# Tokens in residue order: two attention groups score 128 keys instead of 256

## The chip, the cores and the metric

The kernel runs on one core of a Trainium2 chip. The metric is the device time of one execution in microseconds (us), as the median of several runs. The trace shown is of one profiled execution. The engines are TensorE (PE; its weight loads are PEld), VectorE (DVE), ScalarE (ACT), GpSimd (POOL) and SyncE (SP).

## What is computed

A two-layer encoder on 256 tokens of width 1024, in float32. Each layer has a mixer and a feed-forward part; layer 0 has a dense SwiGLU, layer 1 eight experts of which each token uses two. The mixer reads one normalised input through one wide projection into two branches: a recurrence over time (convolution of width 4, then a gated linear scan forward and backward), and attention. In the attention, 12 heads of 64 channels are in three groups of four. Group g has a dilation d and a window: a query at t sees the keys t + j*d.

```python
WINDOWS = (128, 512, 2048)
DILATIONS = (1, 4, 16)
def dilated_band_attention(q, k, v, dilation, half_keys):
    """Query t attends keys t + j*dilation, j in [-half_keys, half_keys]."""
    ...
    s = jnp.einsum('brnqhd,brnkhd->brnhqk', qb, kb) * (HEAD_DIM ** -0.5)
    ...
    s = jnp.where(mask[None, None, :, None, :, :], s, -jnp.inf)
    lse = jax.nn.logsumexp(s, axis=-1)
    ...
mix = jax.nn.softmax(jnp.stack(lses, axis=0), axis=0)
att = jnp.sum(mix[..., None] * jnp.stack(outs, axis=0), axis=0)
```

The three groups are weighed by their denominators, so that slot s (one head of each group) is one softmax over the allowed keys of its three heads. With 256 tokens the two wider windows cut nothing off: their groups see every key of the query's own residue mod 4 or mod 16.

## The kernel before

Tokens lie on partitions in two blocks (TB = 2) of 128, in the order of time. All weights come from HBM as one stream of 1 MB parts into the ring `raw`, loaded by SP. Each part has two halves; a half is split in two for accuracy: ACT writes `w_hi` (L478), DVE the rest `w_lo` (L485), three halves ahead of PE. PE makes three matmuls for each product (`mm3`, L490 to L492: hi by hi, lo, and lo by hi).

The order of all work is one list, `STEPS`, that `schedule()` writes out by hand. Every engine goes through it and does its own share of each step. A step "G" is one half of a product with weights; `at(gap, ...)` puts side steps between the products. The side steps that matter here:

- "tx": PE transposes the recurrence's input, DVE copies it from PSUM into `xT` (L1367). "conv" (L1375, L1382) makes `xc` from `xT` shifted by 0 to 3 tokens; "lg" is the recurrence's gates, fp32 matmuls on `xc` (L994), whose 256 columns per product go to the PSUM tile `mid`. "ls" are the scans (L1414, L1418), whose result goes back to `xT`, and "lf" multiplies it with `gy` (L1431).
- "tq": queries and keys transposed into `qkT`.
- The attention has 8 units a layer, u = token block x slot. "as" is the scores of a unit (L1020): for each of three groups one fp32 matmul, 64-row weights (the 128 queries of the block), all 256 keys as columns, into `mid` (768 columns over two banks). "am": DVE adds the mask `band` and takes the maximum (L1453), ACT takes the exponential with its sum (L802), all on 128x768 in `sm`. "ap" transposes four 128-column pieces of `sm` on PE (L1030), and ACT copies them to `pt` (L808); "aq" transposes the other two, and DVE copies those (L1464) and takes the reciprocal of the sum (L1468). "av" multiplies the six pieces with `v`, six fp32 matmuls of 64 columns (L1043), and DVE scales the result into `att` (L1474).

These stages of different units share a slot between two products: `stages = [("ap", i - 2), ("as", i), ("av", i - 3), ("aq", i - 2), ("am", i)]` (L144). The transposed results of "tn", "tx", "tq", "ap", "aq", "av" and others take turns on two PSUM banks, `turn`, in the order of the list: a step waits until the last but one user of its bank was read. `mid` is single: the scores of a unit wait until the masking pass of the unit before has read it.

The masks are part of the constants that ACT's queue loads at the start (L668): two blocks x three groups x 256 columns, 0 or -1e30.

Of the kernel before, what the change touches and what calls it, by code (L numbers as in the profile page):

```python
# [35 lines left out]
UNITS = TB * SLOTS  # L36
F_DENSE, F_EXP, EXPERTS = 2816, 3584, 8
EPS = 1e-6
SCALE = DH ** -0.5
NEG = -1e30  # L40
# [48 lines left out]
def schedule():  # L89
# [16 lines left out]
    for L in range(DEPTH):  # L106
# [35 lines left out]

        for i in range(UNITS + 3):
            stages = [("ap", i - 2), ("as", i), ("av", i - 3), ("aq", i - 2), ("am", i)]  # L144
            at(20.5 + i / 2, *(s for s in stages if 0 <= s[1] < UNITS))
# [59 lines left out]
def tables():  # L205


    half_at, last_half, pair, freed, kinds = {}, {}, {}, {}, {}

    uses, ring = [0, 0, 0], {2: 0, 3: 1}  # L210
    todo = []
    for L in range(DEPTH):
        todo += [((L, n), k, i, 2) for n, k, i in MIXER]
        if L == 0:
            todo += [((L, n), k, i, 3) for n, k, i in dense_order()]
    for j, (key, kind, i, width) in enumerate(todo):
        half_at[key, i], last_half[key] = 2 * j, 2 * j + 2
        if key not in kinds:
            kinds[key] = kind
            pair[key], freed[key] = [], []  # L220
            for _ in range(2 if kind in "ws" else 1):
                if key[1][0] == "lru":
                    p = 2
                else:
                    p = ring[width] % width
                    ring[width] += 1
                pair[key].append(p)
                freed[key].append(uses[p])
                uses[p] += TB
    turn, n = {}, 0  # L230
    count = {"tn": 2, "tx": 2, "ty": 2, "tq": 1, "ap": 1, "aq": 1, "av": 1, "ta": 1, "tm": 2, "th": 2}
# [14 lines left out]
C_MASK = 4 * P  # L246
C_COS = C_MASK + TB * GROUPS * T
C_SIN = C_COS + TB * 8
# [29 lines left out]
def build(nc, stream, gates_w, x_in, norms, consts_in, vecs_in, out):  # L278
    with ExitStack() as ctx:
        def keep(name, shape, dt=F32, into=ctx):  # L280
            return into.enter_context(nc.sbuf_tensor(name, shape, dt))
# [21 lines left out]
        with ExitStack() as m:  # L303
            sm = keep("sm", [P, 2, GROUPS * T], into=m)
            pt = [keep("pt0", [P, 2 * GROUPS, P], into=m)]
            att = keep("att", [P, TB, T], into=m)
            with ExitStack() as m2:
                pt.append(keep("pt1", [P, 2 * GROUPS, P], into=m2))
            att_hi = keep("att_hi", [P, 2, T], F32R, m)
            att_lo = keep("att_lo", [P, 2, T], F32R, m)  # L310
# [198 lines left out]
        def mid_before(L, use):  # L509


            lru = min(use, 8)
            at_ = use - lru
            return L * 16 + use, L * (8 * 4 + 8) + 4 * lru + at_

        def xslice(n):
# [117 lines left out]
        def _(act):  # L634
# [28 lines left out]
            for s in STEPS:  # L663
# [141 lines left out]
                elif kind == "ap":  # L805
                    idx = TURN[s]
                    bank_full(act, idx)
                    nc.scalar.activation(pt[s[2] % 2][:, 0:4, :],  # L808
                                         turn[idx % 2][:, :].rearrange("p (a t) -> p a t", a=4),
# [89 lines left out]
        def _(pe):  # L899
# [37 lines left out]
            for s in STEPS:  # L937
# [70 lines left out]
                elif kind == "as":  # L1008
                    _, L, u = s
                    b, sl = u // SLOTS, u % SLOTS  # L1010
                    uses, frees = mid_before(L, 8 + u)
                    pe.wait_ge(mid_free, frees)
                    if u == 0:
                        for j in range(4, 6):
                            bank_read(pe, TURN[("tq", L, j)])
                    flat = mid[:, :, :].rearrange("p a c -> p (a c)")
                    for g in range(GROUPS):
                        head = g * SLOTS + sl
                        o = DH * (head % 2)
                        ins = nc.tensor.matmul(flat[:, g * T:(g + 1) * T],  # L1020
                                               qkT[o:o + DH, head // 2, 0, b * P:(b + 1) * P],
                                               qkT[o:o + DH, head // 2, 1, :], start=True, stop=True)
                    ins.then_inc(mid_full, 1)
                elif kind in ("ap", "aq"):

                    _, L, u = s
                    pe.wait_ge(p_ready, 8 * L + u + 1)
                    t_ = turn_bank(TURN[s])
                    for k, c in enumerate(range(4) if kind == "ap" else range(4, 2 * GROUPS)):
                        ins = nc.tensor.transpose(t_[:, k * P:(k + 1) * P], sm[:, u % 2, c * P:(c + 1) * P],  # L1030
                                                  ident)
                    ins.then_inc(turned, 1)
                elif kind == "av":
                    _, L, u = s
                    b, sl = u // SLOTS, u % SLOTS
                    for part in ("ap", "aq"):
                        bank_read(pe, TURN[(part, L, u)])
                    idx = TURN[s]
                    t_ = turn_bank(idx)
                    for i in range(2 * GROUPS):  # L1040
                        g, kb = i // 2, i % 2
                        o = (g * SLOTS + sl) * DH
                        ins = nc.tensor.matmul(t_[:, 0:DH], pt[u % 2][:, i, :], v[:, kb, o:o + DH],  # L1043
                                               start=i == 0, stop=i == 2 * GROUPS - 1)
                    ins.then_inc(turned, 1)
# [154 lines left out]
        def _(dve):  # L1200
# [65 lines left out]
            for s in STEPS:  # L1266
# [94 lines left out]
                elif kind == "tx":  # L1361
                    _, L, c = s
                    for k in range(2):
                        idx = TURN[s] + k
                        n = 4 * c + 2 * k
                        bank_full(dve, idx)
                        nc.vector.tensor_copy(xT[:, n:n + 2, 1:T + 1],  # L1367
                                              turn[idx % 2][:, :].rearrange("p (n t) -> p n t", n=2)
                                              ).then_inc(turn_free[idx % 2], 1)
# [55 lines left out]
                elif kind == "lf":  # L1425
                    _, L, pr = s
                    dve.wait_ge(scanned, scans_done(L, 1, 1))
                    for i in range(2):
                        bank_read(dve, TURN[("ty", L, 1)] + i)
                    y2 = gy[:, 2 * pr:2 * pr + 2, :]  # L1430
                    nc.vector.tensor_tensor(y2, xT[:, 2 * pr:2 * pr + 2, 0:T], y2,  # L1431
                                            ALU.mult).then_inc(lru_full, 1)
# [11 lines left out]
                elif kind == "am":  # L1444
# [4 lines left out]
                    if u >= 2:  # L1449

                        bank_full(dve, TURN[("aq", L, u - 2)])
                    flat = mid[:, :, :].rearrange("p a c -> p (a c)")
                    nc.vector.tensor_tensor_reduce(out=sm[:, u % 2, :], in0=flat[:, 0:GROUPS * T],  # L1453
                                                   in1=band[:, b, :], scale=1.0, scalar=NEG, op0=ALU.add,
# [4 lines left out]
                                            ALU.mult).then_inc(nm_ready, 1)  # L1459
                elif kind == "aq":  # L1460
                    _, L, u = s
                    idx = TURN[s]
                    bank_full(dve, idx)
                    nc.vector.tensor_copy(pt[u % 2][:, 4:6, :],  # L1464
                                          turn[idx % 2][:, 0:2 * P].rearrange("p (a t) -> p a t", a=2)
                                          ).then_inc(turn_free[idx % 2], 1)
                    dve.wait_ge(p_ready, 8 * L + u + 1)
# [251 lines left out]


def constants():

    c = np.zeros((P, C_END), np.float32)
    i = np.arange(P)
    c[:, C_ID:C_ID + P] = np.eye(P)
    c[:, C_IOTA:C_IOTA + P] = i[None, :]
    c[:, C_BEFORE:C_BEFORE + P] = i[:, None] < i[None, :]
    c[:, C_ONES:C_ONES + P] = 1
    k = np.arange(T)
    for b in range(TB):  # L1730
        rel = (b * P + i)[:, None] - k[None, :]
        for g in range(GROUPS):
            ok = (rel % DILATIONS[g] == 0) & (np.abs(rel) <= WINDOWS[g] // 2)
            o = C_MASK + (b * GROUPS + g) * T
            c[:, o:o + T] = np.where(ok, 0, NEG)
        freq = (np.float32(500000.0) ** (-np.arange(0, 16, 2, dtype=np.float32) / np.float32(16))).astype(np.float32)
        ang = (b * P + i)[:, None].astype(np.float32) * freq[None, :]
# [37 lines left out]
```

## Time and profile before

| | us |
|---|---|
| runs, median of 3 | 1754.05 |
| runs, lowest and highest | 1750.28, 1754.47 |
| profiled execution, first to last instruction | 1745.8 |
| PE busy in it | 1695.2 |
| DVE busy | 1410.3 |
| ACT busy | 1223.3 |
| POOL busy | 45.1 |

For the profiled execution the span is what is given; it runs from the first to the last instruction, and a run's device time holds what lies around it as well. An engine's busy time is an average over stages with different limits, so it must be read stage by stage. The attention of layer 0 lies at about 160 to 220 us, that of layer 1 at 600 to 660 us, and the experts take the time from about 720 us to the end.

### The profile page before, as it was taken

What the parts mean: (1) busy time and instruction counts of PE and PEld (TensorE: products, weight loads), DVE (VectorE), ACT (ScalarE), POOL (GpSimd) and SP (SyncE); (2) the same over time, 40 slices, a digit from 0 to 9 for tenths busy, and PEclk for the clock granted to TensorE, in tenths of its full rate; (3) what the DMA queues carried; (4) which work ended last, traced back from release to release, by engine and by line L of the source; (5) the groups of instructions that cost most, each with busy time, mean ns of one, the idle gap of its engine ahead of it and who ended that gap; (6) DMA issues with size and microseconds to landing.
All of it is one profiled execution on the core that took longest, in us unless ns stands there. A gap on an engine that the chain in (4) does not pass through costs nothing.

```text
span 1745.8 us, 24050 instructions
## 1 busy us (share of the span) xinstructions
PE 1695.2 (97%) x7960; PEld 1397.6 (80%) x7960; DVE 1410.3 (81%) x1546; ACT 1223.3 (70%) x1431; POOL 45.1 (3%) x30
## 2 busy tenths in 40 slices
PE   7989999999999999899999999999999999999996
PEld 5877888888887788688888888888888888888885
DVE  5777575565777756699899899899898998998997
ACT  5686545444568754578878878777787877888785
POOL 0130000000003000000000000000000000000000
PEclk9999999999999999899999999999999999999999
DMA  9434255555543324299899899899899998998993
GB/s 366 167 121 145 97 217 205 185 183 187 189 146 136 145 97 168 97 365 371 329 367 368 328 362 375 324 367 371 322 368 347 349 369 339 352 373 326 368 369 137
DMA packets 66120, 471.22 MB, mean 270 GB/s; under 512 B 7312, under 2 KB 7568, under 8 KB 9744
## 3 DMA queue, kind: packets, MB, share of 16 engines
q1 hardware_dynamic: 64768, 462.97, 70.4%
q0 software_dynamic: 864, 6.29, 1.0%
q10 hardware_dynamic: 432, 1.22, 0.2%
q8 instruction: 34, 0.56, 0.1%
q14 instruction: 22, 0.18, 0.0%
HBM read 469.41 MB, written 1.05 MB: 269 GB/s over the span
## 4 chain that ended last, share of the span: by engine, by line
PE 86%; DVE 6%; ACT 5%; issue 2%; DMA 1%; SPq 0%; DVEq 0%; ACTq 0%
PE bank L490 18%; PE bank L492 18%; PE bank L491 18%; PE mid L490 8%; PE mid L492 8%; PE mid L491 8%; PE turn L1118 2%; PE turn L1159 1%; PE mid L1020 1%; PE turn L1043 1%; DVE w_lo L485 1%; DMA raw<-in_stream 1%; ACT w_hi L478 1%; DVE xT L1414 1%; PE mid L994 1%
## 5 line engine op out<-in xcount | busy, mean ns | idle before, releaser
L485 DVE TENSOR_TENSOR w_lo<-raw,w_hi 128x1024 fp32r<-128x1024 f32 x877 | 1069.7, 1234 | 241.4 <-ACT w_hi L478 201.0
L478 ACT ACTIVATE w_hi<-raw 128x1024 fp32r<-128x1024 f32 x877 | 924.3, 1060 | 326.4 <-PE bank L492 194.3
L490 PE MATMUL bank<-w_hi,g_hi 128*128 128x512 f32 x896 | 357.2, 399 | 0.0
L492 PE MATMUL bank<-w_hi,g_lo 128*128 128x512 f32 x896 | 351.3, 392 | 0.0
L491 PE MATMUL bank<-w_lo,g_hi 128*128 128x512 f32 x896 | 351.2, 392 | 0.0
L490 PE MATMUL bank<-w_hi,a_hi 128*128 128x512 f32 (+1 forms) x608 | 242.3, 399 | 14.9 <-DVE w_lo L485 12.2
L492 PE MATMUL bank<-w_hi,a_lo 128*128 128x512 f32 (+1 forms) x608 | 235.0, 387 | 0.0
L491 PE MATMUL bank<-w_lo,a_hi 128*128 128x512 f32 (+1 forms) x608 | 234.5, 386 | 0.0
L490 PEld LDWEIGHTS bank<-w_hi,g_hi 128*128 128x128 f32 x896 | 168.8, 188 | 38.1 <-DVE w_lo L485 3.0
L492 PEld LDWEIGHTS bank<-w_hi,g_lo 128*128 128x128 f32 x896 | 168.5, 188 | 38.1
L491 PEld LDWEIGHTS bank<-w_lo,g_hi 128*128 128x128 f32 x896 | 168.9, 189 | 34.3
L490 PE MATMUL mid<-w_hi,eT_hi 128*128 128x512 f32 x448 | 178.1, 398 | 0.0
L492 PE MATMUL mid<-w_hi,eT_lo 128*128 128x512 f32 x448 | 175.7, 392 | 0.0
L491 PE MATMUL mid<-w_lo,eT_hi 128*128 128x512 f32 x448 | 174.8, 390 | 0.0
L490 PEld LDWEIGHTS bank<-w_hi,a_hi 128*128 128x128 f32 x608 | 116.2, 191 | 40.9 <-issue 15.9
L492 PEld LDWEIGHTS bank<-w_hi,a_lo 128*128 128x128 f32 x608 | 115.9, 191 | 23.4
L491 PEld LDWEIGHTS bank<-w_lo,a_hi 128*128 128x128 f32 x608 | 116.5, 192 | 21.2
L492 PEld LDWEIGHTS mid<-w_hi,eT_lo 128*128 128x128 f32 x448 | 84.1, 188 | 19.1
L491 PEld LDWEIGHTS mid<-w_lo,eT_hi 128*128 128x128 f32 x448 | 84.3, 188 | 17.5
L490 PEld LDWEIGHTS mid<-w_hi,eT_hi 128*128 128x128 f32 x448 | 84.3, 188 | 16.7
L802 ACT ACTIVATE sm<-sm,small 128x768 f32<-128x768 f32 x16 | 15.0, 939 | 45.6 <-DVE small L1458 45.6
L1623 DVE TENSOR_TENSOR eT_lo<-turn,eT_hi 128x512 fp32r<-128x512 f32 x56 | 38.3, 683 | 0.0
(224 smaller groups left out, 1608.0 us busy)
## 6 DMA issues: line engine op xcount, KB each, us to landing
raw<-in_stream SPq DMA_DIRECT2D x438, 1024.0 KB, 4.8
wg<-in_gates POOLq DMA_DIRECT2D x2, 2048.0 KB, 11.8
gain<-in_norms POOLq DMA_DIRECT2D x4, 512.0 KB, 4.0
x<-in_x SPq DMA_DIRECT2D x2, 512.0 KB, 6.0
raw<-in_stream SPq DMA_DIRECT2D x2, 512.0 KB, 6.7
out_x<-xn SPq DMA_DIRECT2D x4, 256.0 KB, 2.1
const<-in_consts ACTq DMA_DIRECT2D x1, 1008.0 KB, 14.0
gain<-in_norms SPq DMA_DIRECT2D x2, 256.0 KB, 7.0
```

The costliest lines, as they stand in the source:

```text
L478: nc.scalar.activation(w_hi[:, h % H, :], raw[:, part % R, lo:lo + HALF], ACT.Copy).then_inc(hi_ready, 1)
L485: nc.vector.tensor_tensor(w_lo[:, h % H, :], raw[:, part % R, lo:lo + HALF], w_hi[:, h % H, :].bitcast(F32), ALU.subtract).then_inc(lo_rea ...
L490: nc.tensor.matmul(out_, s_hi, wh, start=start, stop=False)
L491: nc.tensor.matmul(out_, s_hi, wl, start=False, stop=False)
L492: return nc.tensor.matmul(out_, s_lo, wh, start=False, stop=stop)
L994: ins = nc.tensor.matmul(mid[:, q, g * T:(g + 1) * T], wg[:, d, g, n, :], xc[:, n, :], start=True, stop=True)
L1020: ins = nc.tensor.matmul(flat[:, g * T:(g + 1) * T], qkT[o:o + DH, head // 2, 0, b * P:(b + 1) * P], qkT[o:o + DH, head // 2, 1, :], start ...
L1043: ins = nc.tensor.matmul(t_[:, 0:DH], pt[u % 2][:, i, :], v[:, kb, o:o + DH], start=i == 0, stop=i == 2 * GROUPS - 1)
L1118: ins = nc.tensor.matmul(t_[:, k * P:(k + 1) * P], src[:, b, kt * P:(kt + 1) * P], sel[:, b, :], start=i == 0, stop=i == 2 * TB - 1)
L1159: ins = nc.tensor.transpose(t_[:, k * P:(k + 1) * P], eh[c % 2][:, k * P:(k + 1) * P], ident)
L1414: nc.vector.tensor_tensor_scan(xT[:, n, 0:T], rg[:, n, :], ig[:, n, :], 0.0, ALU.mult, ALU.add).then_inc(scanned, 1)
L1623: nc.vector.tensor_tensor(eT_lo[c % 2][:, :, :], turn[idx % 2][:, :].rearrange("p (k t) -> p k t", k=4), eT_hi[c % 2][:, :, :].bitcast(F32 ...
```

## The change

The host hands the tokens over in another order: all t with t mod 4 = 0 first, then 1, 2, 3 (`token_order`), and puts the output back into the order of time. Block 0 holds residues 0 and 1, block 1 residues 2 and 3. A query of the groups with dilation 4 and 16 then finds all its keys in its own block, so "as" has 256 + 128 + 128 = 512 columns for a unit instead of 768, which is one bank of `mid`; units alternate between the two banks (`att_free`). "am" works on 512 columns, "aq" is gone, "av" has four products, and the mask has 512 columns a block. The rotary tables and the group with dilation 1 follow the new order through tables and mask. The recurrence needs the order of time: "tx" writes `xT` back into it, and "lf" reads it out of it, by an access pattern with a step of four elements (`by_residue`).

```diff
-            stages = [("ap", i - 2), ("as", i), ("av", i - 3), ("aq", i - 2), ("am", i)]
+            stages = [("ap", i - 2), ("as", i), ("av", i - 3), ("am", i)]
...
+        def att_free(L, u):
+
+            return mid_before(L, 8)[1] if u < 2 else mid_before(L, 8 + u - 1)[1]
+
+        def by_residue(a):
+
+            return a.rearrange("p n (j r) -> p n r j", r=RES)
...
-                    nc.scalar.activation(pt[s[2] % 2][:, 0:4, :],
+                    nc.scalar.activation(pt[s[2] % 2][:, :, :],
...
-                    pe.wait_ge(mid_free, frees)
+                    pe.wait_ge(mid_free, att_free(L, u))
...
-                    for g in range(GROUPS):
+                    own = slice(b * P, (b + 1) * P)
+                    for g, keys, o_ in ((0, slice(0, T), 0), (1, own, T), (2, own, T + P)):
                         head = g * SLOTS + sl
                         o = DH * (head % 2)
-                        ins = nc.tensor.matmul(flat[:, g * T:(g + 1) * T],
-                                               qkT[o:o + DH, head // 2, 0, b * P:(b + 1) * P],
-                                               qkT[o:o + DH, head // 2, 1, :], start=True, stop=True)
+                        ins = nc.tensor.matmul(mid[:, u % 2, o_:o_ + keys.stop - keys.start],
+                                               qkT[o:o + DH, head // 2, 0, own],
+                                               qkT[o:o + DH, head // 2, 1, keys], start=True, stop=True)
...
-                    for k, c in enumerate(range(4) if kind == "ap" else range(4, 2 * GROUPS)):
+                    for c in range(KEYS // P):
...
-                    for i in range(2 * GROUPS):
-                        g, kb = i // 2, i % 2
+                    for i, (g, kb) in enumerate(((0, 0), (0, 1), (1, b), (2, b))):
...
-                        nc.vector.tensor_copy(xT[:, n:n + 2, 1:T + 1],
-                                              turn[idx % 2][:, :].rearrange("p (n t) -> p n t", n=2)
+                        nc.vector.tensor_copy(by_residue(xT[:, n:n + 2, 1:T + 1]),
+                                              turn[idx % 2][:, :].rearrange("p (n r j) -> p n r j", n=2, r=RES)
...
-                    nc.vector.tensor_tensor(y2, xT[:, 2 * pr:2 * pr + 2, 0:T], y2,
+                    y4 = y2.rearrange("p n (r j) -> p n r j", r=RES)
+                    nc.vector.tensor_tensor(y4, by_residue(xT[:, 2 * pr:2 * pr + 2, 0:T]), y4,
...
-                        bank_full(dve, TURN[("aq", L, u - 2)])
-                    flat = mid[:, :, :].rearrange("p a c -> p (a c)")
-                    nc.vector.tensor_tensor_reduce(out=sm[:, u % 2, :], in0=flat[:, 0:GROUPS * T],
+                        bank_full(dve, TURN[("ap", L, u - 2)])
+                    nc.vector.tensor_tensor_reduce(out=sm[:, u % 2, :], in0=mid[:, u % 2, :],
...
-                elif kind == "aq":
+                elif kind == "ap":
                     _, L, u = s
-                    idx = TURN[s]
-                    bank_full(dve, idx)
-                    nc.vector.tensor_copy(pt[u % 2][:, 4:6, :],
-                                          turn[idx % 2][:, 0:2 * P].rearrange("p (a t) -> p a t", a=2)
-                                          ).then_inc(turn_free[idx % 2], 1)
+                    if u >= 2:
+                        bank_read(dve, TURN[("av", L, u - 2)])
                     dve.wait_ge(p_ready, 8 * L + u + 1)
                     link(nc.vector.reciprocal(rr[:, u % 2:u % 2 + 1], rs[:, u % 2:u % 2 + 1]))
...
+def token_order():
+
+
+    return np.arange(T).reshape(T // RES, RES).transpose().reshape(T)
```

## Rows read from the trace of the kernel before

**Rows 1.** The page: moved bytes in 40 slices, and the chain of waits

```profile
GB/s 366 167 121 145 97 217 205 185 183 187 189 146 136 145 97 168 97 365 371 329 367 368 328 362 375 324 367 371 322 368 347 349 369 339 352 373 326 368 369 137
...
PE 86%; DVE 6%; ACT 5%; issue 2%; DMA 1%; SPq 0%; DVEq 0%; ACTq 0%
```

**Rows 2.** Windows: busy us of PE, PEld, DVE, ACT, POOL (instructions), PE clock, DMA share, GB/s

```profile
40.00:70.00 30.00, 29.07 (x137) 24.53 (x138) 30.00 (x51) 15.17 (x24) 5.98 (x1) 1.00 0.43 161
160.00:220.00 60.00, 59.60 (x325) 48.41 (x324) 33.57 (x69) 36.24 (x54) 0.00 (x0) 1.00 0.26 92
600.00:660.00 60.00, 59.60 (x326) 48.39 (x325) 33.97 (x68) 36.54 (x54) 0.00 (x0) 1.00 0.26 90
760.00:1740.00 980.00, 971.76 (x4480) 799.29 (x4478) 894.88 (x855) 776.40 (x819) 0.00 (x0) 1.00 0.91 346
```

**Rows 3.** Waits: who waited for whom, us in total, times, longest

```profile
ACT w_hi L478 <- DMA raw<-in_stream: 10.2, 3, 6.9
...
PE turn L1030 <- ACT pt L808: 0.8, 2, 0.4
```

**Rows 4.** Timeline of PE in three attention slots: start, us, instruction

```profile
161.72 0.39 PE L491 MATMUL bank<-w_lo,a_hi 128*128 128x512 f32 x1
161.95 0.39 PE L492 MATMUL bank<-w_hi,a_lo 128*128 128x512 f32 x1
162.26 1.56 PE L1020 MATMUL mid<-qkT 64*128 64x256 f32 x6
...
164.09 0.39 PE L491 MATMUL bank<-w_lo,a_hi 128*128 128x512 f32 x1
...
170.83 0.40 PE L492 MATMUL bank<-w_hi,a_lo 128*128 128x512 f32 x1
...
173.08 0.44 PE L1030 MATMUL turn<-const,sm 128*128 128x128 f32 x2
...
173.59 0.39 PE L491 MATMUL bank<-w_lo,a_hi 128*128 128x512 f32 x1
...
175.89 0.40 PE L492 MATMUL bank<-w_hi,a_lo 128*128 128x512 f32 x1
...
179.99 0.39 PE L491 MATMUL bank<-w_lo,a_hi 128*128 128x512 f32 x1
```

**Rows 5.** The chain in order of time: start, us on the chain, what

```profile
62.75 1.73 PE mid L994 x8
...
845.34 1.73 PE turn L1118 x16
```

**Rows 6.** Groups by line: busy us, mean ns, idle before

```profile
L1453 DVE CUSTOM_DVE_ANT_0 sm<-mid,const 128x768 f32<-128x768 f32 x16 | 15.3, 958 | 0.4
...
L1418 DVE TENSOR_TENSOR_SCAN root<-rg,ig 128x256 f32<-128x256 f32 x16 | 9.7, 670 | 0.0
...
L1367 DVE COPY xT<-turn 128x512 f32<-128x512 f32 x8 | 5.1, 682 | 0.8 <-PE turn L981 0.8
```

**Rows 7.** DMA issues (KB each, us to landing), and ACT's timeline at the start

```profile
const<-in_consts ACTq DMA_DIRECT2D x1, 1008.0 KB, 14.0
...
23.38 1.06 ACT L478 ACTIVATE w_hi<-raw 128x1024 fp32r<-128x1024 f32 x1 [6.87 <-DMA raw<-in_stream]
```

**Rows 8.** Timelines of DVE and PE: convolutions and the gates that take them

```profile
45.56 2.46 DVE L1382 SCALAR_TENSOR_TENSOR xc<-xT,vec,xc 128x256 f32<-128x256 f32 x6
...
52.05 2.46 DVE L1382 SCALAR_TENSOR_TENSOR xc<-xT,vec,xc 128x256 f32<-128x256 f32 x6
...
48.21 1.89 PE L994 MATMUL mid<-xc,wg 128*128 128x256 f32 x8
...
55.39 1.89 PE L994 MATMUL mid<-xc,wg 128*128 128x256 f32 x8
...
489.51 2.46 DVE L1382 SCALAR_TENSOR_TENSOR xc<-xT,vec,xc 128x256 f32<-128x256 f32 x6
...
494.29 1.89 PE L994 MATMUL mid<-xc,wg 128*128 128x256 f32 x8
```

More of the change, by code:

```diff
@@ L36 @@
 UNITS = TB * SLOTS
+KEYS = T + 2 * P
+RES = 4
 F_DENSE, F_EXP, EXPERTS = 2816, 3584, 8
@@ L230, in tables @@
     turn, n = {}, 0
-    count = {"tn": 2, "tx": 2, "ty": 2, "tq": 1, "ap": 1, "aq": 1, "av": 1, "ta": 1, "tm": 2, "th": 2}
+    count = {"tn": 2, "tx": 2, "ty": 2, "tq": 1, "ap": 1, "av": 1, "ta": 1, "tm": 2, "th": 2}
     for s in STEPS:
@@ L246 @@
 C_MASK = 4 * P
-C_COS = C_MASK + TB * GROUPS * T
+C_COS = C_MASK + TB * KEYS
 C_SIN = C_COS + TB * 8
@@ L303, in build @@
         with ExitStack() as m:
-            sm = keep("sm", [P, 2, GROUPS * T], into=m)
-            pt = [keep("pt0", [P, 2 * GROUPS, P], into=m)]
+            sm = keep("sm", [P, 2, KEYS], into=m)
+            pt = [keep(f"pt{i}", [P, KEYS // P, P], into=m) for i in range(2)]
             att = keep("att", [P, TB, T], into=m)
-            with ExitStack() as m2:
-                pt.append(keep("pt1", [P, 2 * GROUPS, P], into=m2))
             att_hi = keep("att_hi", [P, 2, T], F32R, m)
@@ L1010, in _ @@
                     b, sl = u // SLOTS, u % SLOTS
-                    uses, frees = mid_before(L, 8 + u)
-                    pe.wait_ge(mid_free, frees)
+                    pe.wait_ge(mid_free, att_free(L, u))
                     if u == 0:
@@ L1015, in _ @@
                             bank_read(pe, TURN[("tq", L, j)])
-                    flat = mid[:, :, :].rearrange("p a c -> p (a c)")
-                    for g in range(GROUPS):
+                    own = slice(b * P, (b + 1) * P)
+                    for g, keys, o_ in ((0, slice(0, T), 0), (1, own, T), (2, own, T + P)):
                         head = g * SLOTS + sl
                         o = DH * (head % 2)
-                        ins = nc.tensor.matmul(flat[:, g * T:(g + 1) * T],
-                                               qkT[o:o + DH, head // 2, 0, b * P:(b + 1) * P],
-                                               qkT[o:o + DH, head // 2, 1, :], start=True, stop=True)
+                        ins = nc.tensor.matmul(mid[:, u % 2, o_:o_ + keys.stop - keys.start],
+                                               qkT[o:o + DH, head // 2, 0, own],
+                                               qkT[o:o + DH, head // 2, 1, keys], start=True, stop=True)
                     ins.then_inc(mid_full, 1)
-                elif kind in ("ap", "aq"):
+                elif kind == "ap":
                     _, L, u = s
@@ L1028, in _ @@
                     t_ = turn_bank(TURN[s])
-                    for k, c in enumerate(range(4) if kind == "ap" else range(4, 2 * GROUPS)):
-                        ins = nc.tensor.transpose(t_[:, k * P:(k + 1) * P], sm[:, u % 2, c * P:(c + 1) * P],
+                    for c in range(KEYS // P):
+                        ins = nc.tensor.transpose(t_[:, c * P:(c + 1) * P], sm[:, u % 2, c * P:(c + 1) * P],
                                                   ident)
@@ L1035, in _ @@
                     b, sl = u // SLOTS, u % SLOTS
-                    for part in ("ap", "aq"):
-                        bank_read(pe, TURN[(part, L, u)])
+                    bank_read(pe, TURN[("ap", L, u)])
                     idx = TURN[s]
                     t_ = turn_bank(idx)
-                    for i in range(2 * GROUPS):
-                        g, kb = i // 2, i % 2
+                    for i, (g, kb) in enumerate(((0, 0), (0, 1), (1, b), (2, b))):
                         o = (g * SLOTS + sl) * DH
                         ins = nc.tensor.matmul(t_[:, 0:DH], pt[u % 2][:, i, :], v[:, kb, o:o + DH],
-                                               start=i == 0, stop=i == 2 * GROUPS - 1)
+                                               start=i == 0, stop=i == KEYS // P - 1)
                     ins.then_inc(turned, 1)
@@ L1449, in _ @@
                     if u >= 2:
-                        bank_full(dve, TURN[("aq", L, u - 2)])
-                    flat = mid[:, :, :].rearrange("p a c -> p (a c)")
-                    nc.vector.tensor_tensor_reduce(out=sm[:, u % 2, :], in0=flat[:, 0:GROUPS * T],
+                        bank_full(dve, TURN[("ap", L, u - 2)])
+                    nc.vector.tensor_tensor_reduce(out=sm[:, u % 2, :], in0=mid[:, u % 2, :],
                                                    in1=band[:, b, :], scale=1.0, scalar=NEG, op0=ALU.add,
@@ L1459, in _ @@
                                             ALU.mult).then_inc(nm_ready, 1)
-                elif kind == "aq":
+                elif kind == "ap":
                     _, L, u = s
-                    idx = TURN[s]
-                    bank_full(dve, idx)
-                    nc.vector.tensor_copy(pt[u % 2][:, 4:6, :],
-                                          turn[idx % 2][:, 0:2 * P].rearrange("p (a t) -> p a t", a=2)
-                                          ).then_inc(turn_free[idx % 2], 1)
+                    if u >= 2:
+                        bank_read(dve, TURN[("av", L, u - 2)])
                     dve.wait_ge(p_ready, 8 * L + u + 1)
@@ L1728, in constants @@
     c[:, C_ONES:C_ONES + P] = 1
-    k = np.arange(T)
+    token = token_order()
     for b in range(TB):
-        rel = (b * P + i)[:, None] - k[None, :]
-        for g in range(GROUPS):
+        o = C_MASK + b * KEYS
+        here = token[b * P:(b + 1) * P]
+        for g, keys in ((0, token), (1, here), (2, here)):
+            rel = here[:, None] - keys[None, :]
             ok = (rel % DILATIONS[g] == 0) & (np.abs(rel) <= WINDOWS[g] // 2)
-            o = C_MASK + (b * GROUPS + g) * T
-            c[:, o:o + T] = np.where(ok, 0, NEG)
+            c[:, o:o + len(keys)] = np.where(ok, 0, NEG)
+            o += len(keys)
         freq = (np.float32(500000.0) ** (-np.arange(0, 16, 2, dtype=np.float32) / np.float32(16))).astype(np.float32)
-        ang = (b * P + i)[:, None].astype(np.float32) * freq[None, :]
+        ang = here[:, None].astype(np.float32) * freq[None, :]
         c[:, C_COS + 8 * b:C_COS + 8 * b + 8] = np.cos(ang)
@@ L1764 @@
         "stream": weight_stream(inp), "gates": np.ascontiguousarray(gates),
-        "x": inp["x"].reshape(T, D), "norms": norms, "consts": constants(),
+        "x": np.ascontiguousarray(inp["x"].reshape(T, D)[token_order()]), "norms": norms, "consts": constants(),
         "vecs": np.ascontiguousarray(vecs),
@@ L1773 @@
     r = run_bass_kernel_spmd(nc, [{f"in_{k}": a for k, a in arrays.items()}], core_ids=[0])
-    return r.results[0]["out_x"].reshape(1, T, D)
+    return r.results[0]["out_x"].reshape(RES, T // RES, D).transpose(1, 0, 2).reshape(1, T, D)
```

## The prediction

> **What bounds the kernel now.** I read the page's chain of waits first, then the windows by stage, then TensorE's timeline inside the attention, then the waits. The chain that ended last is TensorE for 86% of the span [rows 1]: a microsecond of TensorE work that goes is a microsecond of time, unless it lay where something else leads. So the question is what leads where the change acts. It acts in four places, and the windows give each of them [rows 2]. In both attention stretches (160 to 220 us in layer 0, 600 to 660 us in layer 1) PE is busy 59.60 us of 60 at a granted clock of 1.00, while DVE has 33.6 and 34.0 us of work and ACT 36.2 and 36.5, and the DMA engines are 0.26 busy: TensorE alone sets the pace. From 760 us on, in the experts, PE is busy 971.8 of 980 us, so what is won earlier is carried to the end. ACT waits there for PE, and for the weight stream only 10.2 us in the whole run, in three waits [rows 3]. From 40 to 70 us it is otherwise: DVE is busy 30.00 of 30 us, and the copies into xT stand there.
>
> **TensorE in the attention.** An attention unit is one head slot of one token block; 8 units a layer, 16 in all. Products (the "G" steps) and attention steps alternate on PE, so I take each attention step's cost from how far apart the products around it start. Two product matmuls start 0.23 us apart when nothing is between (161.72 and 161.95) [rows 4]. With only scores between, L492 at 161.95 and L491 at 164.09 are 2.14 us apart; less two such steps of 0.23 the scores cost 1.68 us. With 4 transposes, scores and 2 transposes it is 170.83 to 173.59, so 2.76 - 0.46 = 2.30 us: six transposes cost 0.62, or 0.103 each. The full slot is 175.89 to 179.99, so 3.64 us, which leaves 3.64 - 2.30 = 1.34 us for the 12 records of "av" (six products), 0.112 each. An fp32 product shows as two records (x6 for three scores), a transpose as one.
>
> What goes, per unit:
> - Two of six transposes (the whole "aq" step on PE): 2 x 0.103 = 0.21 us.
> - Two of six products of "av": 4 records, 4 x 0.112 = 0.45 us; at the 0.108 of the next point it is 0.43. I take 0.44.
> - Scores: three products of 256 key columns become one of 256 and two of 128. A record of 256 columns costs 1.73 / 8 = 0.216 us (L994) [rows 5]. So 6 x 0.216 = 1.30 of the 1.68 us is columns, and 0.38 is a fixed part around them, which I let stay. What an fp32 record of 128 columns costs isn't in the trace. Bounds: 0.103 (the transpose, 128 columns) and 0.216 (as if columns did not matter). The row nearest in shape is L1118, 128x128 weights against 128 columns: 1.73 / 16 = 0.108 [rows 5]. "av", with half those columns, costs 0.112 and not 0.054, so about 0.11 is a floor, and the floor is where half of 0.216 lies. I take 0.108: 4 x (0.216 - 0.108) = 0.43 us; with the bounds 0 to 0.45.
>
> Sum: 0.21 + 0.44 + 0.43 = 1.08 us a unit, x16 = 17.3 us. Besides, PE stood idle 0.8 us in two waits of its transposes for ACT's pt copy, which held the turn bank of "aq" [rows 3]; with "aq" gone, each "ap" finds its bank read a slot ago: 0.8 us.
>
> **Who must keep up.** Per unit, DVE loses its pt copy and a third of the masking pass L1453 (0.96 us for 768 elements) [rows 6], ACT a third of the exponential; ACT's copy into pt stays at 128x512. All of that was cover, and is worth nothing while PE leads; it is the reason why they follow. PE's 60 us shrink to about 51, and DVE's 34 and ACT's 36 shrink as well. The waits: "as" now waits for the masking pass of two units earlier, not one (looser). The mask pass waits for the transposes "ap", issued before the scores, instead of "aq", issued last in the slot (looser). One wait is added: DVE at "ap" for its own L1474 of unit u-2, with the reciprocal, the att scaling and the mask pass behind it; that instruction ran one slot before on the same engine, so it costs nothing. The reciprocal needs the sums of the exponential two slots back.
>
> **The start.** The masks shrink from 2 x 768 to 2 x 512 columns, 128 x 512 x 4 B = 256 KB of the 1008 KB of the constants' load [rows 7]. That load is in flight when ACT waits 6.87 us for a stream part, until 23.38 us, the longest of its three waits [rows 7], and the first slice of the page moves 366 GB/s [rows 1]. 256 KB at 366 GB/s is 0.7 us. I take all of it; the bounds are 0 and 0.7.
>
> **The copies into xT and the reads from it.** The 4 copies a layer, L1367 (0.682 us each) [rows 6], now write every fourth element (16 B apart); L1431 reads so in 4 passes a layer. No DVE row of this trace has such a step. Below, it costs nothing, as a contiguous copy (and gains nothing, the elements being the same). Above, I take the slowest DVE row by element that has no other engine beside it, the scan L1418 with 0.670 us for 256 elements [rows 6]: 512 at that rate are 1.34 us, 0.66 more than now. In layer 0 the first xc is ready at 45.56 + 2.46 = 48.02 and PE takes it at 48.21; the next, behind all four copies, at 54.51 for 55.39 [rows 8]. Four times 0.66 is 2.64, less the 0.88 to spare: PE 1.76 us late. In layer 1 the second place has 494.29 - 491.97 = 2.32 us to spare [rows 8]: 0.32 late. L1431 has DVE's idle 26 us of each attention stretch as its cover; without it, it would add up to 0.66 x 8 = 5.3 us. So 0 to 2.1 us, and I take 0.3: a copy is nearer to a copy than to a scan. The Trainium skill speaks against the change here: "SBUF — State Buffer", the note on cachelines in the section "Door 1: The DMA port swizzle", says a line is 16 bytes and each access that crosses to a new line pays a penalty, without a figure; four fp32 elements is just that step. By it the penalty would fall on every element; no run here shows it yet.
>
> **Sum.** 17.3 + 0.8 + 0.7 - 0.3 = 18.5 us. The profiled execution has a span of 1745.8 us; the median of the runs is 1754.05, 8.2 us outside the span, which the change doesn't touch. 1754.05 - 18.5 = 1735.5 us.
>
> **Rivals.**
> - *128 key columns cost as much as 256* (0.216 a record). For it: "av" shows that records don't shrink without end. Against: that floor is 0.11. It gives 18.5 - 6.9 = 11.6 us: 1742.4.
> - *ACT leads at the end of the attention.* ACT's table load, four sigmoids, last g0 eviction and its splits stand close together there, and PE comes to this place sooner. Against: the exponential before it starts sooner too, and over the whole stretch ACT has 23 us to spare [rows 2]. If PE lost 2 us there in each layer: 1739.5.
> - *The gain is given back in the experts*, if the stream of weights led there: DMA share is 0.91 [rows 2]. Against: PE is busy 0.99 of it. It gives about 1754, at best the start's 0.7 less.
> - *Slower: the 16 B step makes DVE's copies many times longer.* DVE has no gap from 40 to 70 us, so the extra e of each copy goes to PE: 4e - 0.9 in layer 0, 4e - 2.3 in layer 1. This eats the 18.8 us of gain from e = 2.75 us, a copy of 3.4 us, five times now; beyond it the kernel is slower, with a copy of 4.2 us (e = 3.5) by 24.8 - 18.8 = 6.0 us: 1760. For it: no row shows such a step, and DVE has no cover there. Against: five times is far from any DVE row without another engine beside it, the scan is at twice. By the rule of the Trainium skill named above a penalty is certain and its size open; the trace of before cannot say.
>
> **How the numbers follow.** The forecast as summed, 1731 to 1739: 0.77. 128 columns at full price: 0.10. ACT at the end of attention: 0.05. Given back: 0.05. Slower: 0.03. The terms alone span 1734.8 (0.103 a record, nothing lost in the copies) to 1744.9 (0.216 a record, 2.1 lost, nothing from the start); the runs of before lie within 4.2 us, 2 us to either side. So 1731 to 1744 holds the forecast and the first two rivals. About 0.3%, 5.3 us, is what a measurement of this kernel tells from no change. Faster by more 0.92, within 0.05, slower 0.03.
>
> **What the profile after would show.** Scores as six records still, four of 128 columns; a full slot of 3.64 - 1.08 = 2.56 us between products; "av" x8 in 0.9 us; PE busy without a gap in both attention stretches, each some 8.7 us shorter; L1453 near 0.69 us; L1367 at 0.68, or longer if the step costs. The prediction is wrong if the 128-column records show 0.2 us apart, if PE waits for DVE at L994 between 45 and 60 us, or if PE has gaps in the attention that it has not now.

## The result and the profile after

The changed kernel takes 1735.6 us (median of 4 runs, 1733.24 to 1737.14) against 1753.26 us of the kernel before (4 runs, 1750.28 to 1754.47): a ratio of 0.9907, with a 95% interval from 0.9895 to 0.9919. That is 17.7 us less, where 18.5 were forecast (1735.5 us).

The windows of the kernel after, columns as in [rows 2]. The attention stretches are now some 164 to 213 and 597 to 645 us:

```profile
40.00:70.00 30.00, 28.62 (x134) 23.99 (x135) 30.00 (x49) 15.33 (x23) 6.62 (x1) 1.00 0.44 158
160.00:212.00 52.00, 52.00 (x282) 42.85 (x281) 28.82 (x59) 32.97 (x52) 0.00 (x0) 1.00 0.33 121
590.00:640.00 50.00, 50.00 (x263) 40.95 (x262) 27.79 (x56) 28.86 (x47) 0.00 (x0) 0.98 0.32 110
760.00:1700.00 940.00, 940.00 (x4325) 773.77 (x4324) 864.16 (x821) 750.26 (x785) 0.00 (x0) 1.00 0.93 355
```

PE is busy 52 of 52 and 50 of 50 us there, now without the 0.40 us gap that each layer had in [rows 2, 3]; in 52 us DVE works 28.8 and ACT 33.0. TensorE still leads, and leads in the experts too.

One full attention slot in PE's timeline of the kernel after, with the last product before it and the first two behind it:

```profile
181.90 0.40 PE L492 MATMUL bank<-w_hi,a_lo 128*128 128x512 f32 x1
182.13 0.60 PE L1037 MATMUL turn<-const,sm 128*128 128x128 f32 x4
182.66 1.14 PE L1027 MATMUL mid<-qkT 64*128 64x256 f32 x6
183.73 1.10 PE L1048 MATMUL turn<-v,pt 128*128 128x64 f32 x8
184.65 0.48 PE L490 MATMUL bank<-w_hi,a_hi 128*128 128x512 f32 x1
184.96 0.39 PE L491 MATMUL bank<-w_lo,a_hi 128*128 128x512 f32 x1
```

By the reckoning of the prediction the slot costs 184.96 - 181.90 - 0.46 = 2.60 us, where it was 3.64 in [rows 4]: 1.04 less. Scores take 1.07 us until "av" starts. A full slot of before, in its timeline:

```profile
176.65 1.56 PE L1020 MATMUL mid<-qkT 64*128 64x256 f32 x6
178.14 1.55 PE L1043 MATMUL turn<-v,pt 128*128 128x64 f32 x12
179.53 0.39 PE L1030 MATMUL turn<-const,sm 128*128 128x128 f32 x2
179.67 0.47 PE L490 MATMUL bank<-w_hi,a_hi 128*128 128x512 f32 x1
```

Scores were 1.49 and are 1.07 us; "av" was 1.39 and is 0.92; the two transposes were 0.14. From the first scores to the product behind the last "av" the attention of layer 0 took 162.26 to 219.46, 57.20 us, and takes 164.39 to 212.67, 48.28 us; layer 1 took 601.54 to 658.74, also 57.20, and takes 596.53 to 644.78, 48.25. That is 8.9 us a layer, 17.9 in all.

The groups by line of the kernel after that answer to [rows 6], the read of lf beside them (it was 0.69 us):

```profile
L1458 DVE CUSTOM_DVE_ANT_0 sm<-mid,const 128x512 f32<-128x512 f32 x16 | 10.9, 683 | 0.1
L1437 DVE TENSOR_TENSOR gy<-xT,gy 128x512 f32<-128x512 f32 x8 | 8.7, 1084 | 0.0
L1372 DVE COPY xT<-turn 128x512 f32<-128x512 f32 x8 | 8.0, 1078 | 0.8 <-PE turn L989 0.8
```

The stepped copy takes 1.08 us instead of 0.68, 0.40 more; the stepped read the same.

PE's timeline of the kernel after at the first transposes of "tx" and the gate products that wait for their convolutions, answering to [rows 8]:

```profile
41.10 1.09 PE L989 MATMUL turn<-const,xn 128*128 128x128 f32 x8 [1.21 <-DVE xn L1319]
47.51 1.03 PE L989 MATMUL turn<-const,xn 128*128 128x128 f32 x8
48.82 1.99 PE L1002 MATMUL mid<-xc,wg 128*128 128x256 f32 x8 [0.28 <-DVE xc L1387]
56.12 1.89 PE L1002 MATMUL mid<-xc,wg 128*128 128x256 f32 x8
63.30 1.89 PE L1002 MATMUL mid<-xc,wg 128*128 128x256 f32 x8
```

PE now waits for DVE at L1002, a wait that before did not have, and it is at the first gate product, behind two of the four copies: there the kernel before had xc ready 0.19 us ahead of PE (48.02 for 48.21 in [rows 8]). From the transposes (40.93, then 41.10) to the fourth gate product (69.79, then 70.50) it was 28.86 us and is 29.40: 0.54 later, of which 0.44 are there at the first gate product already (48.21 - 40.93 = 7.28 and 48.82 - 41.10 = 7.72). In layer 1 the same way is 28.82 us in both.

The profiled execution of the kernel after has a span of 1733.6 us, only 12.2 less than 1745.8. Stage by stage, with the same landmarks on PE in both traces, the 12.2 us are these: the two attentions take 17.9 us less, and 5.7 us are given back elsewhere, 0.2 before the first transposes, 0.5 from there to the fourth gate product, 1.4 in layer 0 and 1.8 in layer 1 between the fourth gate product and the first scores, and 1.8 from the last "av" of layer 1 to the end. The last three vary from execution to execution: the trace of before_again (the kernel before once more, below) has 94.64 and 94.60 us between fourth gate product and first scores, where the first trace of before has 92.47 and 92.85 and that of after 93.89 and 94.61, and from the first gather of the experts to the end it takes 1023.7 us, the first trace 1021.6 and that of after 1023.2. The attention itself repeats: 57.17 to 57.20 us in both traces of the kernel before, 48.24 to 48.28 in all nine traces of the kernel after and its variants. So the two spans show only 12.2 of the 17.7 us because the trace of before is of a quick execution.

### The profile page after: what moved, and what is told of

Its sections match the earlier page's. It is cut to its first block, busy times and chain, and to the rows that moved or that the text cites. A ratio compares the mean times of both kernels' runs of the same rounds, so it can differ in the third digit from the quotient of the medians.

```text
span 1733.6 us, 23848 instructions
## 1 busy us (share of the span) xinstructions
PE 1681.6 (97%) x7864; PEld 1387.1 (80%) x7864; DVE 1405.5 (81%) x1530; ACT 1220.6 (70%) x1431; POOL 48.8 (3%) x30
## 4 chain that ended last, share of the span: by engine, by line
PE 86%; DVE 6%; ACT 4%; issue 2%; DMA 1%; SPq 0%; DVEq 0%; ACTq 0%
PE bank L490 18%; PE bank L492 18%; PE bank L491 18%; PE mid L490 8%; PE mid L492 8%; PE mid L491 8%; PE turn L1123 2%; PE turn L1164 1%; DVE w_lo L485 1%; DMA raw<-in_stream 1%; DVE xT L1419 1%; PE mid L1027 1%; ACT w_hi L478 1%; PE turn L1048 1%; PE mid L1002 1%
## 5 line engine op out<-in xcount | busy, mean ns | idle before, releaser
L1620 DVE TENSOR_TENSOR eh<-bank,eh 128x512 f32<-128x512 f32 x56 | 38.2, 683 | 0.0
```

Source lines behind the costliest of these rows:

```text
L1620: nc.vector.tensor_tensor(eh[c % 2][:, :], bank[2 * (c % 2) + 1][:, :], eh[c % 2][:, :], ALU.mult).then_inc(e_hid, 1)
```

## The experiments

Kernels whose name begins with b_ are the kernel before with one edit, those with a_ the kernel after with one. Ratios are to the kernel before on the same chip.

**before_again: the kernel before once more.**

> The kernel before, unchanged, to see the span and the granted clock of each of its runs. The four runs of the changed kernel took 1.9 us more than their spans. If that holds here too, a run of 1753 us has a span near 1751, and the trace of before (1745.8) was a quicker execution than the median, because TensorE's clock dipped less in it (0.991). Rival: 8 us lie outside the span of the kernel before, and the change took some of them away.

1753.0 us (12 runs, 1748.76 to 1755.76), ratio 0.9997 (0.9988 to 1.0007). In every run the time is 1.8 to 1.9 us more than the span, so the rival is out. The spans spread with the clock. Of the 42 runs of the kernel before that were timed beside the kernels from before_again to a_copies_x3, the 16 with a mean clock of 0.990 took 1750.3 us on average, the 6 with 0.988 took 1752.6, the 15 with 0.987 took 1753.7, the 5 with 0.986 took 1754.8. The first trace, with 0.991 and 1745.8, is quicker than all of these: with 1.9 us it makes 1747.7, which is 5.6 below the median of 1753.26, while the profiled execution of the kernel after (1735.5) is at its median. That is why the spans differ by 12.2 and the medians by 17.7. So the "8.2 us outside the span" of the prediction was wrong: 1.9 us lie outside, and the rest is that the profiled execution was quicker than the median. It did no harm, as the gain was taken off the median.

Where the clock differs is seen, for one, in three windows of the kernel before (columns as in [rows 2]):

```profile
90.00:95.00 5.00, 1.48 (x7) 0.95 (x6) 4.14 (x4) 2.70 (x6) 4.92 (x5) 1.00 0.00 0
95.00:100.00 5.00, 5.00 (x28) 4.39 (x28) 4.53 (x2) 4.98 (x8) 4.30 (x3) 1.00 0.62 213
100.00:105.00 5.00, 5.00 (x42) 4.96 (x41) 2.79 (x4) 4.96 (x8) 0.00 (x0) 1.00 0.57 210
```

and the same of the kernel after:

```profile
90.00:95.00 5.00, 1.48 (x8) 0.93 (x6) 4.83 (x4) 2.00 (x5) 4.92 (x4) 0.89 0.00 0
95.00:100.00 5.00, 5.00 (x12) 3.94 (x13) 3.84 (x2) 4.14 (x7) 4.99 (x3) 0.50 0.61 211
100.00:105.00 5.00, 5.00 (x34) 4.63 (x33) 2.87 (x3) 4.48 (x7) 0.00 (x0) 0.92 0.53 185
```

In both, PE has only 1.48 us of work from 90 to 95 us. Behind it the clock stayed at 1.00 (2.4 GHz) in the one execution. In the other it stood at 0.50 (1.2 GHz) from 95 to 100 us, with 12 instructions done where there had been 28, and the means of 0.89 and 0.92 beside it put another 2 us or so at that level. The stretch from the fourth gate product of layer 0 to the first scores is 1.4 us longer in this trace; that the clock did it is inferred from these windows. A shorter fall lies in the window from 590 us shown above (mean clock 0.98). The fall varies with the execution, for the same work of 1.48 us from 90 to 95 us: the window from 95 to 100 us has 0.66 in the trace of after_again, 0.67 in a_contig and 0.55 in a_psum_read.

**b_scores128: only the scores narrowed.**

```diff
-                        ins = nc.tensor.matmul(flat[:, g * T:(g + 1) * T],
+                        own = slice(b * P, (b + 1) * P) if g else slice(0, T)
+                        ins = nc.tensor.matmul(flat[:, g * T + own.start:g * T + own.stop],
                                                qkT[o:o + DH, head // 2, 0, b * P:(b + 1) * P],
-                                               qkT[o:o + DH, head // 2, 1, :], start=True, stop=True)
+                                               qkT[o:o + DH, head // 2, 1, own], start=True, stop=True)
```

> The kernel before, with one thing changed: the scores of the groups with dilation 4 and 16 are matmuls of 128 key columns, not 256 (the other 128 columns keep what was there; no token order is changed, so half of these groups' keys are left out). If TensorE's records alone set the time: 16 units x 4 records x (0.216 - 0.108) = 6.9 us less, near 1746.5. If the gain of the whole change comes rather from less work on VectorE and ScalarE and from looser waits, which are all as before here: no change, 1753.

1747.97 us (12 runs), ratio 0.9977 (0.9968 to 0.9986): 2.5 to 5.6 us less, not 6.9. A full slot is 5.99 us from scores to scores (185.60 to 191.59) where it was 6.41, so the term itself is there, 0.42 us. But the stretch from first scores to the last "av" fell by 2.3 us a layer, from 55.95 to 53.64. Its timeline on PE shows why:

```profile
179.29 1.14 PE L1021 MATMUL mid<-qkT 64*128 64x256 f32 x6 [0.26 <-DVE small L1454]
...
200.47 0.41 PE L1031 MATMUL turn<-const,sm 128*128 128x128 f32 x2 [0.27 <-ACT pt L808]
...
211.74 0.41 PE L1031 MATMUL turn<-const,sm 128*128 128x128 f32 x2 [0.38 <-ACT pt L808]
```

With the masking pass still 768 wide and `mid` single, the scores of unit 3 wait for DVE (0.26), in the same slot "aq" comes 1.70 us behind "av" instead of 1.39, and "aq" waits twice for ACT's copy, where before it did so once. From product to product the two slots in which this is new take 4.33 us (178.20 to 182.53) and 4.13 (196.81 to 200.94); with 0.43 off their lengths of before, 4.10 and 4.16, they would be 3.67 and 3.73. That is 1.06 of the 1.1 us that are missing to 8 x 0.43. DVE and ACT had been so close behind PE that a part of the gain turned into waits. In the whole change these waits do not arise, since it also relaxes what they wait for.

**b_no_aq: no "aq", four products in "av".**

```diff
-            stages = [("ap", i - 2), ("as", i), ("av", i - 3), ("aq", i - 2), ("am", i)]
+            stages = [("ap", i - 2), ("as", i), ("av", i - 3), ("am", i)]
...
-                    for i in range(2 * GROUPS):
+                    for i in range(4):
                         g, kb = i // 2, i % 2
```

> The kernel before, without the aq step and without two of the six products of av (the last group's keys are left out of the sum). The scores, mask and exponential stay 768 wide. If the terms add up: 16 x (0.21 + 0.44) + 0.8 = 11.2 us less, near 1742, and with b_scores128 together the 18 us. If something else leads once PE is shorter, clearly less than 11.

1741.35 us (5 runs), ratio 0.9931 (0.9919 to 0.9944): 9.8 to 14.2 us less, with 11.2 forecast. In the trace the stretch to the start of the last "av" is 50.83 us instead of 55.95, to which the shorter last "av" adds 0.45: 5.6 us a layer, 11.1 in all. The two parts by themselves give 2.3 + 5.1 = 7.4 us of that stretch, the whole change 55.95 - 47.48 = 8.5; the 1.1 us are the two slots named above.

**The copies.** b_strided has the stepped patterns alone:

> The kernel before, with only the access patterns with a step of four elements in the copies into xT and the reads of lf (the recurrence then sees its tokens in another order). In the trace of the changed kernel these cost VectorE 0.40 and 0.39 us more each. By the room found in the trace of before, 4 x 0.40 - 0.88 = 0.7 us slower in layer 0 and nothing in layer 1: near 1754. Rival: VectorE is full from 40 to 70 us and all of it goes to TensorE, 8 x 0.40 = 3.2 us, or with the reads 6.4 us slower.

1754.58 us (11 runs), ratio 1.0013 (1.0003 to 1.0022): 0.5 to 3.9 us slower. In the trace, PE's way from the transposes to the fourth gate product is 41.40 to 70.81, 29.41 us, in layer 0 and 28.82 in layer 1, just as in the kernel after: 0.5 us late in layer 0, and nothing in layer 1. The reads of lf lie under PE's work, since the attention stretches are 56.07 us, 0.12 longer than before. That all of the 6.4 us went to TensorE is excluded by both. The 3.2 us of the copies alone lie inside the interval of the times; it is the trace that excludes them. Whether the rest of the median's 2 us is real stays open; none of the 11 runs reached the clock of 0.990, which 16 of 42 did before.

a_contig takes the step away from the kernel after:

> The changed kernel with the copies into xT and the reads of lf contiguous again (the recurrence then runs in residue order, which is not what the reference computes). If the step of four elements costs time only where the copies have no room: 0.5 to 0.7 us faster than the changed kernel, near 1735. If the strided passes cost all that they are longer: 3 to 6 us faster, near 1730.

1734.63 us (4 runs), ratio 0.9891 (0.9875 to 0.9908). The way is 28.88 us again (40.99 to 69.87). By the medians it is 1.0 us from the kernel after, within what the runs spread, and far from 3 to 6.

a_copies_x3 makes the cost large, to find what the room is worth:

```diff
+                        for rep in range(2):
+                            link(nc.vector.tensor_copy(by_residue(xT[:, n:n + 2, 1:T + 1]),
+                                                       turn[idx % 2][:, :].rearrange("p (n r j) -> p n r j", n=2,
+                                                                                     r=RES)))
```

> The changed kernel with each strided copy into xT done three times, so that each costs VectorE 0.40 + 2 x 1.08 = 2.56 us more than a contiguous one. By the room of 0.88 us in layer 0 and 2.32 us in layer 1: 4 x 2.56 - 0.88 = 9.4 and 4 x 2.56 - 2.32 = 7.9 us late, less the 0.7 us that the changed kernel loses already: 16.6 us slower than it, near 1752, so that the kernel would be back at the time of before. If VectorE's delay is taken up elsewhere (it has idle time from 71 us on): a few us only.

1751.38 us (10 runs), 15.8 us above the kernel after, and at the time of before (0.9993, 0.9983 to 1.0003). On the way from transposes to the fourth gate product layer 0 takes 40.52 to 78.76, 9.4 us more than with contiguous copies, as forecast; layer 1 takes 480.35 to 518.63, 38.28 us, 9.5 more where 7.9 were expected, and some of it comes back later, since both layers together would make 18.4 us more than in the kernel after, and the time shows 15.8. So the place of the slower rival was right: what DVE loses there beyond its room is lost by PE. Only the price, 0.40 us a copy and not 2.75, keeps the change on the good side.

How the price depends on the step, from one execution each:

> The changed kernel with a step of two elements (8 bytes) instead of four in the copies into xT and the reads of lf (the recurrence's order is then wrong). If the price hangs on how many elements are taken from each 16 bytes, two of four should bring the copy near the contiguous 0.68 us. If any step costs: 1.08 us as with four.

> The changed kernel with a step of eight elements (32 bytes) in the same places. If the price is paid once for each element that lies in another 16 bytes than the one before, it is the same as with four: 1.08 us. If it grows with the distance: more, 1.5 us or so.

The two lines of a_step2, at a step of two elements (its time was 1731.36 us):

```profile
L1437 DVE TENSOR_TENSOR gy<-xT,gy 128x512 f32<-128x512 f32 x8 | 5.5, 692 | 0.0
L1372 DVE COPY xT<-turn 128x512 f32<-128x512 f32 x8 | 5.1, 682 | 0.8 <-PE turn L989 0.8
```

and of a_step8, at eight (1734.14 us):

```profile
L1437 DVE TENSOR_TENSOR gy<-xT,gy 128x512 f32<-128x512 f32 x8 | 9.4, 1179 | 0.0
L1372 DVE COPY xT<-turn 128x512 f32<-128x512 f32 x8 | 8.6, 1160 | 0.8 <-PE turn L989 0.8
```

In the copy (step on the write) a step of 8 bytes is free, one of 16 bytes costs 0.40 us for 512 elements (0.8 ns an element), one of 32 bytes 0.48; the pass of lf (step on the read) shows the same within 0.01 us. This agrees with the Trainium skill ("SBUF — State Buffer", the note on cachelines in "Door 1: The DMA port swizzle"): two elements of each 16 bytes are enough for full speed, and with one there is a penalty. The small rise from 16 to 32 bytes is not in that rule.

**a_psum_read: the same result, the step on the other side.**

```diff
-                        nc.vector.tensor_copy(by_residue(xT[:, n:n + 2, 1:T + 1]),
-                                              turn[idx % 2][:, :].rearrange("p (n r j) -> p n r j", n=2, r=RES)
+                        nc.vector.tensor_copy(xT[:, n:n + 2, 1:T + 1].rearrange("p n (j r) -> p n j r", r=RES),
+                                              turn[idx % 2][:, :].rearrange("p (n r j) -> p n j r", n=2, r=RES)
```

> The changed kernel, computing the same: the copies into xT write four neighbouring tokens at a time and take the step (64 elements) on the PSUM side. If the penalty belongs to the side in SBUF that is stepped through, the copy is back at 0.68 us and the time as with contiguous copies, near 1735. If a stepped read of PSUM costs as much or more, the copy is at 1.08 us or above and nothing is won.

1733.41 us (4 runs), ratio 0.9884 (0.9867 to 0.9900). Its line:

```profile
L1372 DVE COPY xT<-turn 128x512 f32<-128x512 f32 x8 | 5.1, 683 | 0.8 <-PE turn L989 0.8
```

A copy that reads PSUM with a step of 256 bytes and writes neighbours costs no more than a contiguous one. It was timed again beside the kernel after:

> The changed kernel again, to be held against the version beside it on the same chip: 1735 to 1736.

> The changed kernel with the copies into xT stepping on the PSUM side, timed again. In the traces the fourth gate product comes 28.86 us after the first transposes with contiguous copies and 29.40 us with strided ones, in layer 0 alone. So 0.5 us faster than the changed kernel if that delay is all; 2 us faster, as the medians of the first timing have it (1733.4 against 1735.6), if the delay also moves TensorE's idle stretches into a costlier place for the clock.

after_again: 1733.73 us (1732.46 to 1734.48), ratio 0.9891 (0.9875 to 0.9908). psum_again: 1733.01 us (1731.39 to 1735.26), ratio 0.9891 (0.9874 to 0.9908). The medians are 0.7 us apart, and the traces say 0.5 us (28.87 against 29.40 on the way in layer 0); four runs each cannot tell that from nothing. It costs nothing either, so it is the version to keep.

**a_full_consts: the old width of the constants.**

```diff
-C_COS = C_MASK + TB * KEYS
+C_COS = C_MASK + TB * 768
```

> The changed kernel with the constants' load at its old width (256 KB of unused columns added). If the smaller load brings the stream part forward, as the prediction had it: 0.7 us slower, near 1736.3, and the wait that ended at 23.56 us ends near 24.2. If the load is hidden: the same time.

1735.96 us (4 runs), ratio 0.9897 (0.9881 to 0.9914), 0.4 or 2.2 us above the two timings of the kernel after. The wait ended at 24.30 us. One trace says little, as this time moves from execution to execution; but all traces together do. The first transposes of "tx", which come behind it, start at 40.93, 43.06, 43.05, 42.17, 41.40 and 41.85 us in the six traces with 1008 KB of constants, on average 42.08, and at 41.10, 40.63, 40.52, 40.99, 40.61, 41.74, 40.42 and 40.59 in the eight with 752 KB, on average 40.83. That is 1.2 us, with a standard error of 0.4 from the spread of both sets, so the 0.7 of the forecast is not excluded. Five of the six with 1008 KB are of the kernel before and its variants; the one of the kernel after, a_full_consts, has 41.85.

## Why the prediction was right

- *TensorE leads in the attention, and goes on leading.* Shown: PE without a gap in both stretches, and each edit that took PE work off there lowered the time. The margin was thinner than the busy shares said (b_scores128 turned part of its gain into waits). The prediction had called the waits of the scores and of the masking pass looser without a price, and priced only the 0.8 us in which PE stood already. What the parts lose apart and the whole does not is 1.1 us a layer.
- *Size per unit.* Forecast 0.21 + 0.44 + 0.43 = 1.08 us; measured 0.14 + 0.47 + 0.42 = 1.03. The 128-column fp32 record was the unknown. Scores fell by 0.42 us for four of them, so each costs 0.105 less than one of 256 columns, 0.111: the choice of 0.108 was right and the rival of full price wrong. The transposes were taken too dear, 0.103 each where the two cost 0.07 each behind "av": the first four of a slot take 0.53 us (176.12 to 176.65), 0.13 each, so the mean over six was not the price of the two that go. The two idle waits of 0.4 us are gone as forecast. In all 17.9 us from first scores to the product behind the last "av", where 18.1 were forecast; 16 x 1.03 + 0.8 makes 17.3 of it. Most of the other 0.6 lies in the slot with the idle wait:

```profile
207.95 0.40 PE L492 MATMUL bank<-w_hi,a_lo 128*128 128x512 f32 x1
...
210.47 0.41 PE L1030 MATMUL turn<-const,sm 128*128 128x128 f32 x2 [0.40 <-ACT pt L808]
...
210.94 0.39 PE L491 MATMUL bank<-w_lo,a_hi 128*128 128x512 f32 x1
```

It takes 2.99 us from product to product, where the next one, with the same steps and no wait, takes 2.42 (213.23 to 215.65): the wait cost 0.57 us and not the 0.40 shown as idle. Layer 1 has the same. One more slot of each layer (195.09 to 199.25) was 0.06 us longer than its neighbours.

- *The start.* 0.7 us forecast, about 1.2 over all traces. In the one trace after, nothing was to be seen of it (23.56 against 23.38 us in [rows 7]).
- *The copies.* 0.3 us taken within 0 to 2.1; measured 0.54, from 0.40 us a copy. The formula gives 4 x 0.40 - 0.88 = 0.72, but at the wrong place: it sums four copies against the room of the second gate product, while PE is held at the first, behind two copies, where the room is 0.19. By durations that would make 2 x 0.40 - 0.19 = 0.61; the pair of copies takes 1.96 us instead of 1.28 there, 0.68 more and not 0.80. This wait is one of the three signs by which the prediction was to be called wrong (PE waiting for DVE at L994, now L1002, between 45 and 60 us). It came, with 0.28 us idle; as the sum had allowed up to 2.1 us for just this, the sign contradicted the 0.3 that was chosen and not the rest. The lf reads are hidden but for 0.1 us a layer in b_strided.
- *The base.* The 8.2 us outside the span was wrong (1.9), without effect on the forecast. The 1754.05 us that the gain was taken from is a median of three runs; with the 1753.26 of the four the same gain makes 1734.8.
- *ACT at the end of the attention; gain given back in the experts.* Neither occurred: between the scores and the last "av" PE waits nowhere for ACT any more, and in the chain of waits the time from the first gather products of the experts to the last but one was 993.1 us (724.22 to 1717.35) and is 993.8 (710.40 to 1704.20).

17.9 + 1.2 - 0.5 = 18.6 us by the traces. That the forecast comes within 0.1 of it is luck in part: the attention was taken 0.2 too high, the start 0.5 too low and the copies 0.2 too cheap, and these cancel. The same holds for 1735.5 against 1735.6: a gain taken 0.8 too high met a base taken 0.8 too high. The first timing gives 14.2 to 18.4 us by its ratio's interval, the second (after_again) 16.1 to 21.9; the two medians are 17.7 and 19.5 us below theirs of before.

## What to carry to other kernels

Where one engine has no gap and the others are half idle, a slot's cost is read from how far apart its neighbours start, once with and once without the step in question; that gave each of the three parts of a unit to within 0.07 us. Ask at the same time how far behind the next engines are: a part of the same change done alone can lose a third of its gain (2.3 us came of 3.4 a layer) to waits that the whole change removes. And when a delay is set against the room at a later place, look at the room of every place before it too. Compare two spans only with the clock and several traces of each beside them: here 5.5 of 17.7 us were missing between two single traces.

## What was not expected of the hardware

A VectorE copy that writes fp32 in SBUF with a step of 16 bytes takes 1.08 us for 512 elements, with 8 bytes 0.68, with 32 bytes 1.16; a step of 256 bytes on the PSUM operand of a copy costs nothing (0.683 us). And after the same idle stretch of PE (1.48 us of work in 5) the clock stayed at full speed in one execution and fell to half for some 7 us in another. The runs of one kernel spread with their mean clock: 1750.3 us on average at 0.990, 1754.8 at 0.986.
